# Moving the last merge's loads, the rotary rotation and the routing scores in a diffusion trunk on one Trainium2 core

## What is computed

```python
h = rmsnorm(x, g_pre1) * (1.0 + sc1) + sh1          # sh, sc, g: from silu(c) @ w_ada + b_ada
dq, dk, dv, sz, sxbc, sdt, nq, nk, nv = split_in(h @ w_in)
o_da = diff_attention(apply_axial_rope(dq), concat([ck, apply_axial_rope(dk)]), concat([cv, dv]), lam)
o_ssm = ssm_branch(...)                              # a state space branch
o_na = neighbourhood_attention(nq, nk, nv, ...)
ga, gs, gn = split(sigmoid(h @ w_gate), 3)
mix = (ga * (o_da @ w_br_da) + gs * (o_ssm @ w_br_ssm) + gn * (o_na @ w_br_na)) @ w_out
x = x + g1 * rmsnorm(mix, g_post1)
h2 = rmsnorm(x, g_pre2) * (1.0 + sc2) + sh2
s = sigmoid(h2 @ w_router)                           # 32 experts, the best 4 of a token are taken
x = x + g2 * rmsnorm(moe_ffn(h2), g_post2)           # routed experts and one shared expert

def rot_half(x, cos, sin):                           # on halves of 32: 16 frequencies for the row, 16 for the column
    x1, x2 = split(x, 2)
    return concat([x1 * cos - x2 * sin, x2 * cos + x1 * sin])
```

## Time and profile before

| | us |
|---|---|
| median of 3 runs | 2616.13 |
| lowest and highest | 2613.88, 2620.17 |
| the profiled execution | 2614.22 |
| its span | 2612.5 |
| PE busy | 2406.2 |
| DVE busy | 949.7 |
| ACT busy | 629.8 |
| POOL busy | 403.7 |

### The profile page before, as it was taken

The page is one execution under the profiler, slowest core; times in us unless marked ns, Lnnn a source line. Parts: engine busy times, 40 slices in busy tenths (PEclk is TensorE's granted clock), DMA queues, the critical chain, the costliest instruction groups (busy, mean ns, idle before and its releaser), DMA issues. The chain is left out here.

```text
span 2612.5 us, 36229 instructions
## 1 busy us (share of the span) xinstructions
PE 2406.2 (92%) x13804; PEld 1439.5 (55%) x13804; DVE 949.7 (36%) x1850; ACT 629.8 (24%) x1519; POOL 403.7 (15%) x456
## 2 busy tenths in 40 slices
PE   5999999989999999899779999998999999989995
PEld 2445644466557655555445565545655765555552
DVE  1423411473106423522364143137410642452226
ACT  2223401350015003122132252016001510312221
POOL 0003100021002300133410030000300230013333
PEclk7999999999999999899879999999999999999998
DMA  8443146100544030589653221220022403155985
GB/s 318 160 162 122 65 149 224 43 1 33 169 145 115 33 125 23 200 332 405 241 218 125 86 94 40 84 73 1 33 89 81 129 33 110 39 204 207 377 343 215
DMA packets 170173, 368.55 MB, mean 141 GB/s; under 512 B 38564, under 2 KB 52140, under 8 KB 170036
## 3 DMA queue, kind: packets, MB, share of 16 engines
q1 hardware_dynamic: 121876, 261.49, 27.4%
q10 hardware_dynamic: 24480, 54.76, 6.0%
q0 software_dynamic: 23680, 50.43, 5.9%
HBM read 344.19 MB, written 47.56 MB: 150 GB/s over the span
## 5 line engine op out<-in xcount | busy, mean ns | idle before, releaser
L228 PE MATMUL ps<-hT,ring 128*128 128x512 f32 x512 | 230.9, 605 | 6.3 <-PEq L1147 2.7
L2513 PE MATMUL ps<-ring,mixT 128*32 128x256 f32 x2688 | 214.0, 382 | 2.9 <-DMA ring<-in_w_e_up 2.5
L237 PE MATMUL ps<-ring,hT 128*128 128x512 f32 x480 | 211.9, 598 | 5.1 <-PEq L1191 4.1
L2513 PEld LDWEIGHTS ps<-ring,mixT 128*32 128x32 f32 x2688 | 120.3, 111 | 95.7 <-issue 21.8
L228 PEld LDWEIGHTS ps<-hT,ring 128*128 128x128 f32 x512 | 96.7, 193 | 130.4 <-issue 130.2
L237 PEld LDWEIGHTS ps<-ring,hT 128*128 128x128 f32 x480 | 90.5, 192 | 115.5 <-issue 113.6
L1278 PE MATMUL ps<-late,ring 128*128 128x320 f32 x512 | 147.2, 447 | 7.6 <-PEq L1366 3.9
L2391 PE MATMUL ps<-ring,mixT 128*128 128x512 f32 x320 | 142.1, 603 | 9.2 <-DVE out_xn L2680 4.8
L1278 PEld LDWEIGHTS ps<-late,ring 128*128 128x128 f32 x512 | 99.6, 196 | 52.9 <-issue 14.8
L1229 POOL TENSOR_TENSOR mix_S<-ring 128x512 f32<-128x512 f32 x16 | 25.2, 1577 | 651.1 <-POOLq L1366 550.1
L664 PE MATMUL ps<-hT,ring 128*128 128x512 f32 x256 | 114.5, 601 | 2.9 <-ACT ssm_dec L916 2.9
(11 more groups left out here) (475 smaller groups left out, 4164.1 us busy)
## 6 DMA issues: line engine op xcount, KB each, us to landing
ring<-in_w_in SPq DMA_DIRECT2D x18, 2048.0 KB, 9.8
ring<-in_w_gate SPq DMA_DIRECT2D x12, 2048.0 KB, 10.1
ring<-in_w_e_down SPq DMA_DIRECT2D x48, 512.0 KB, 17.2
ring<-in_w_e_gate SPq DMA_DIRECT2D x40, 512.0 KB, 5.3
ring<-in_w_e_up SPq DMA_DIRECT2D x40, 512.0 KB, 6.6
co_yg<-y_rows SPq DMA_DIRECT2D x40, 512.0 KB, 5.3
mixT<-in_w_ada ACTq DMA_DIRECT2D x8, 2048.0 KB, 8.7
da_ada_w<-in_w_ada ACTq DMA_DIRECT2D x8, 2048.0 KB, 8.8
```

The source lines that it names most:

```text
L228: pe.matmul(lat, wide[:, k, c], hT[:, k, CTX:TOK], start=(k == 0), stop=(k == kt_n - 1))
L237: last = pe.matmul(out, cx.hT[:, k, tok(t)], wide[:, k, :], start=(k == 0), stop=(k == KT - 1))
L2513: ins = pe.matmul(ps[rows, 2 + b, 0:2 * P].rearrange("p (g f) -> p g f", g=2), xT[:, b, k, rows], ew[:, :, k, :], start=(k == 0), stop=(k ...
```

## The change

- Rotary: the matrix `cx.rot` and its matmuls are gone. DVE shuffles the partitions itself (`stream_shuffle` with `HALF_TURN`, which exchanges the halves of each 32), and the sign is in the sine table. DVE waits for ACT's copy of the chunk (`da_lat_out`).
- Loads: `x`, the gate rows and both sets of modulation parts are allocated before the last merge (`m.post`, `m.own_mods`, `m.mods`) and loaded by SP at the start of it, ahead of the ring sections; SP waits for them at the end of that block. `stage_tail` loads bias and gain only. `stage_combine` uses `m.post` as two of its eight row buffers.
- Scores: the router columns are the stationary side, 32 wide, in four column groups side by side (k and k + 4 in one group); 128 tokens move. ACT copies the four partial sums (`router_out`), and a matmul with a constant `fold` adds them and turns them back (`router_fold`); the fold of a tile stands at the next tile's scores, that of the last behind its `rows_low`.

The diff, without the lines that only rename buffers in `stage_combine` and the constants in `trunk`:

```diff
@@ -48,6 +48,7 @@
 MASKED = -1.0e30
+HALF_TURN = [(i + 16) % 32 for i in range(32)]
...
@@ -122,7 +117,8 @@
         ang[p] = at * inv[d % 16]
-    rope = np.concatenate([np.cos(ang), np.sin(ang)], axis=1).astype(np.float32)
+    sign = np.where(t % 32 < 16, -1.0, 1.0)[:, None]
+    rope = np.concatenate([np.cos(ang), sign * np.sin(ang)], axis=1).astype(np.float32)
     mask = np.zeros((P, NBLK, NKEY), np.float32)
...
@@ -1179,7 +1175,7 @@
-def stage_mix(nc, cx, L, n, branch, g0):
+def stage_mix(nc, cx, L, n, branch, g0, m=None, x=None):
...
@@ -1217,7 +1213,19 @@
         @block.sync
         def _(sp):
+            if x is not None:
+                for g in range(2):
+                    sp.dma_start(m.post[:, g, :], cx.gate_rows[L, 0, g:g + 1, :].broadcast_to([P, D])).then_inc(
+                        name("gate_in"), 16)
+                load_x(cx, sp, L, x, name("x_in"))
+                load_mods(cx, sp, L, 1, m.own_mods, name("mods_in"))
+                if L + 1 < DEPTH:
+                    load_mods(cx, sp, L + 1, 0, m.mods, name("mods_in"))
             load_behind(cx, sp, L, ("gate", g0), ("gate", g0 + 1))
+            if x is not None:
+                sp.wait_ge(name("gate_in"), 32)
+                sp.wait_ge(name("x_in"), 32)
+                sp.wait_ge(name("mods_in"), 160 if L + 1 < DEPTH else 80)
         @block.gpsimd
...
@@ -1440,12 +1448,6 @@
                     pe.wait_ge(sem("da_mm"), n + 1)
                     pe.sem_inc(cx.ring_free, 1)
-                if n >= 2:
-
-                    src = (qT if n - 2 < 4 else kT)[:, (n - 2) % 4, -LAT:]
-                    if n >= 4:
-                        pe.wait_ge(sem("da_sin"), n - 3)
-                    pe.matmul(ps[:, 4 + n % 2, :], cx.rot, src, start=True, stop=True).then_inc(sem("da_rot"), 1)
                 if n == 7:
                     ada.fold(pe, 6)
...
@@ -1497,12 +1499,6 @@
                     ada.fold(pe, 7)
-                if t < 2:
-                    n = 8 + t
-                    pe.wait_ge(sem("da_lat_out"), n - 1)
-                    pe.wait_ge(sem("da_sin"), n - 3)
-                    pe.matmul(ps[:, 4 + n % 2, :], cx.rot, kT[:, n - 6, -LAT:], start=True, stop=True).then_inc(
-                        sem("da_rot"), 1)
                 if t == 0:
...
@@ -1674,9 +1670,10 @@
             def rope_chunk(n):
                 x = (qT if n < 4 else kT)[:, n % 4, -LAT:]
-                dve.wait_ge(sem("da_rot"), n + 1)
+                dve.wait_ge(sem("da_lat_out"), n + 1)
                 r = rt[:, n % 2, :]
-                dve.tensor_tensor(r, ps[:, 4 + n % 2, :], rope[:, 1, :], ALU.mult).then_inc(sem("da_sin"), 1)
+                step(dve, dve.stream_shuffle(r, x, HALF_TURN))
+                dve.tensor_tensor(r, r, rope[:, 1, :], ALU.mult)
                 step(dve, dve.tensor_tensor(x, x, rope[:, 0, :], ALU.mult))
                 dve.tensor_tensor(x, x, r, ALU.add).then_inc(sem("da_roped"), 1)
...
@@ -2208,9 +2205,9 @@
         xn = m.rest
-        mods = Mods(sb("out_mods", [P, 184]))
+        mods = m.own_mods
         ms = sb("out_ms", [P, 6, TILES])
-        gpost = sb("out_gpost", [P, 2, D])
+        gpost = m.post
         shsilu = sb("route_silu", [P, TOK])
...
@@ -2268,11 +2265,8 @@
         def _(sp):
-            load_gate(cx, sp, L, 0, gpost, xn[:, 3, :], xn[:, 4, :], sem("gate_in"))
-            load_x(cx, sp, L, x, sem("x_again"))
-            load_mods(cx, sp, L, 1, mods, sem("mods_in"))
-            if L + 1 < DEPTH:
-                load_mods(cx, sp, L + 1, 0, m.mods, sem("co_mods_in"))
+            sp.dma_start(xn[:, 3, :], w["b_ada"][L:L + 1, 2 * D:3 * D].broadcast_to([P, D])).then_inc(sem("gate_in"), 16)
+            sp.dma_start(xn[:, 4, :], w["g_post1"][L:L + 1].broadcast_to([P, D])).then_inc(sem("gate_in"), 16)
             sp.dma_start(wr[:, :, :], w["w_router"][bass.ds(L, 1)].rearrange("l (p k) n -> p (l k) n", k=KT)).then_inc(
...
@@ -2404,12 +2398,21 @@
                 if t == 0:
                     pe.wait_ge(sem("router_in"), 48)
+                else:
+                    router_fold(t - 1)
                 pe.wait_ge(sem("h_low"), t + 1)
                 pe.wait_ge(sem("h_high"), t + 1)
                 for k in range(KT):
-                    ins = pe.matmul(ps[:, 7, t * NE:(t + 1) * NE], cx.hT[:, k, tok(t)], wr[:, k, :], start=(k == 0),
-                                    stop=(k == KT - 1))
+                    j = k % 4
+                    ins = pe.matmul(ps[NE * j:NE * j + NE, 7, 3 * P:4 * P], wr[:, k, :], cx.hT[:, k, tok(t)],
+                                    start=(k < 4), stop=(k >= 4))
                 ins.then_inc(sem("router_mm"), 1)
+
+            def router_fold(t):
+
+                pe.wait_ge(sem("router_parts"), t + 1)
+                pe.matmul(ps[:, 7, t * NE:(t + 1) * NE], hid[:, t % 2, :], cx.fold[:, 0:NE], start=True,
+                          stop=True).then_inc(sem("router_sums"), 1)
             def rows_low(t):
...
@@ -2462,6 +2465,7 @@
             rows_low(TILES - 1)
+            router_fold(TILES - 1)
             shared_ctx(1)
...
@@ -2569,6 +2573,13 @@
+            def router_out(t):
+
+                act.wait_ge(sem("router_mm"), t + 1)
+                if t >= 2:
+                    act.wait_ge(sem("router_sums"), t - 1)
+                act.activation(hid[:, t % 2, :], ps[:, 7, 3 * P:4 * P], ACT.Copy).then_inc(sem("router_parts"), 1)
+
             for t in range(TILES):
...
@@ -2583,6 +2594,8 @@
                     modulate(t - 1)
+                if t >= 2:
+                    router_out(t - 2)
                 act.wait_ge(sem("x1_ready"), t + 1)
...
@@ -2591,7 +2604,9 @@
             rows_low(TILES - 2)
-            act.wait_ge(sem("router_mm"), TILES)
+            router_out(TILES - 2)
+            router_out(TILES - 1)
+            act.wait_ge(sem("router_sums"), TILES)
             act.activation(s[:, :, :].rearrange("p t e -> p (t e)"), ps[:, 7, 0:TILES * NE], ACT.Sigmoid).then_inc(
...
@@ -2663,16 +2678,14 @@
-            dve.wait_ge(sem("gate_in"), 64)
+            dve.wait_ge(sem("gate_in"), 32)
             finish_gate(cx, dve, gpost, xn[:, 3, :], xn[:, 4, :])
             ins.then_inc(sem("spare_rows"), 1)
-            dve.wait_ge(sem("mods_in"), 80)
             finish_mods(cx, dve, 1, mods).then_inc(sem("mods_known"), 1)
             dve.wait_ge(sem("mods_known"), 1)
-            dve.wait_ge(sem("x_again"), 32)
             for t in range(TILES):
...
@@ -3076,7 +3090,6 @@
             if more:
-                dve.wait_ge(sem("co_mods_in"), 80)
                 finish_mods(cx, dve, 0, m.mods).then_inc(sem("co_mods"), 1)
...
@@ -3213,15 +3226,18 @@
                 stage_na(nc, cx, L)
                 close_passed()
-                stage_mix(nc, cx, L, 1, "n", 4)
+                m = Cx()
                 x = mid.enter_context(nc.sbuf_tensor(f"x_{L}", [P, TILES, D], F32))
+                m.mods = Mods(mid.enter_context(nc.sbuf_tensor(f"next_mods_{L}", [P, 184], F32)))
+                m.own_mods = Mods(mid.enter_context(nc.sbuf_tensor(f"out_mods_{L}", [P, 184], F32)))
+                m.post = mid.enter_context(nc.sbuf_tensor(f"out_gpost_{L}", [P, 2, D], F32))
+                stage_mix(nc, cx, L, 1, "n", 4, m, x)
                 retire_half()
                 cx.half = ExitStack()
                 link = ExitStack()
-                for name in ("co_gains", "co_mods_in", "y_stored0", "y_stored1"):
+                for name in ("co_gains", "y_stored0", "y_stored1"):
                     cx.shared_sems[name] = link.enter_context(nc.semaphore(f"{name}_{L}"))
-                m = Cx()
                 m.hsh = mid.enter_context(nc.sbuf_tensor(f"shared_hidden_{L}", [P, 2, TOK], F32))
                 m.wsd = mid.enter_context(nc.sbuf_tensor(f"shared_down_{L}", [P, 2, D], F32))
```

## The result

The change brought the median from 2617.7 us (17 runs beside it) to 2597.75 us (17 runs, 2590.2 to 2616.0). The ratio is 0.9934, with a 95% interval of 0.992 to 0.9947: 17 us less, between 14 and 21; the plain difference of the medians is 19.9 us. I had forecast 2595 us, 21.1 us less than before, and a range of 2590.5 to 2601. Measured again later beside the last experiment, the ratio was 0.9925 (0.9907 to 0.9943).

A forecast was written before the change was run, and what follows sets the result against it. TensorE, busy 92% of the span, was taken as the bound. Rotary 12.3 + loads 7.6 + scores 1.2 = 21.1 us off the profiled 2614.2 gave 2593.1, forecast as a 2595 us median; range 2590.5 to 2601.

The forecast's parts named there:

- Rotary, second layer: Differential attention's projections, second layer: eight rotation matmuls removed at 0.86 us each, nothing else late; 6.9 us saved.
- Rotary, first layer: First layer's projections, where modulation-weight loads limit the gain: 5.4 us saved, bounds 1.7 and 6.9.
- the step with two transfers: First layer, load behind a ring section already holding PE 1.76 us: two rotations save 0 to 0.95, taken 0.5.
- Rival (a): First layer's transfers take back its rotations: 3.7 us less gain, 2599 us; chance 15%.
- Loads: Output projection's first tiles: earlier loads end PE's stops of 3.83 and 1.00 us and a slow clock; 7.6 us saved.
- its 2.72 us: First layer's output tiles: 16 instructions at granted clock 0.50 take 9.86 us instead of 7.14; 2.72 us saved.
- Scores: Routing scores packed in four column groups: 0.6 us a layer, 1.2 saved in all; bounds loss 2, gain 3.5.
- Shuffle: Added 128x512 shuffle a chunk on DVE in the projections: 0.69 us, hidden under PE, cost nothing.
- Rival (d): Shuffle bounds the projections from 6.3 us, eats the whole gain above 8.0; 2639 us at 10; chance 2%.
- rival (b): Bare table switch behind the score copies costs more than its row: 2.8 us less gain, 2598 us; chance 4%.
- Rival (c): Bias and gain rows still gate DVE, so PE stops at the tail as before: 7.6 us less, 2603; chance 6%.
- D: Follow-up theory on the missing 8 us: the change brings the slow clock, or moved loads slow work above them.

The follow-up runs named there:

- e2: Kernel before the change with the moved loads alone; 2611.3 us, ratio 0.9992.
- e3: Kernel before the change with the packed scores alone; 2614.0 us, ratio 0.9996.
- e12: Changed kernel measured once more, beside e11, nothing edited; 2598.5 us, ratio 0.9925 to the kernel before.
- e1: Kernel before the change with the rotary part alone (shuffle on VectorE, no rotation matmuls); 2602.2 us, ratio 0.9944.
- e4: Changed kernel with a one-column Sigmoid behind the output tiles' last square root, so the table loads there; 2600.1 us, ratio 0.9932.
- e9: Changed kernel; first layer's branch-weight ring section issued only after the eighth, last modulation-weight load has landed; 2595.95 us, ratio 0.9915.
- e10: e9 plus the early Sigmoid table of e4, with the last scores' fold ahead of four transposes on TensorE; 2590.9 us, ratio 0.9892.
- e11: e9 plus the early Sigmoid table of e4, last fold left where the change had it; 2589.9 us, ratio 0.9902.
- e5: Changed kernel; first layer's branch-weight ring section issued only after the sixth modulation-weight load has landed; 2600.2 us, ratio 0.9939.
- e6: Changed kernel with the early Sigmoid table of e4 and the later ring section of e5 together; 2594.5 us, ratio 0.9922.

## Why the prediction was right, and where it was not

The range held the time, and the middle missed by 2.8 us. Part of that nearness is luck: by the ratio the change saved 17 us where I had 21.1, and no term of mine knew of the slow starts behind gaps. Term by term, with all profiles that have the part:

**Rotary, second layer: 6.9 us forecast, 6.7 measured.** 109.20 to 109.24 us in all kernels with the plain shuffle, 115.92 to 115.95 in those without. The 0.2 is not one wait: the 0.30 us hand-over at the fifth chunk stands in before too. By pitch four of the eight rotations gave 0.85 to 0.86 us and one 0.94, but three only 0.78, since the row behind a hand-over takes 0.08 us longer and is now a projection or a value tile.

**Rotary, first layer: 5.4 forecast, 3.3 measured; this is the step that failed.** From the second product of modulation weights, ahead of all eight rotations, to the unit scores: 117.41, 117.15 and 117.40 us without the shuffle (before, e2, e3); 113.74, 113.86, 113.73 and 114.85 with it (after, e12, e1, e4). That is 117.3 against 114.0, 2.3 to 3.7 from pair to pair. For the step with two transfers I took half of the 0.95 us; the two took 14.5 us as before, so nothing was saved there. What I had not reckoned at all was the clock: the stop at this product was 1.48 to 1.76 us and is now 3.24 to 3.62, and each of these was followed by a slow product, 3.09 to 3.64 us instead of 1.92, which gave back up to 1.7 us more. This was also one of the prediction's own signs of being wrong, a lower clock in a place where it was full before. Rival (a) named the cause and priced the stage at 1.7 us; the measured 3.3 lies between it and my 5.4. With the section out of the way (e9, e10, e11: 108.50, 108.72, 109.07) the whole of the rotations comes through: 117.3 - 108.8 = 8.5 us, against 6.9 for them and 1.76 for the stop of before. These are single executions; the timed runs are too wide to show it alone.

**Loads: 7.6 forecast, 6.0 measured.** The mechanism was right, the stop is gone in all 22 places and nothing new is late. Mis-sized is the clock: its 2.72 us, and a term that I had at nothing. I read it from one execution as the price of the long stop; of the three profiles with the stop in the first layer only before's had it (its stop was 3.83 us, the others' 2.47 and 2.60 with full clock behind). Means over the table: first layer 39.7 with the stop, 35.0 without; second 36.8 and 35.5. That is 4.7 and 1.3, 6.0 us in all, uncertain by the few executions with the stop. Against 34.4 us, full clock and no stop, the stops cost 5.3 and 2.4 us, 7.7 together, about what I forecast though in other shares than my 6.55 and 1.00. The missing 1.7 are the slow starts, 0.6 and 1.1 us as means: while PE stopped for DVE anyway, the stop ended 31.5 to 32.0 us behind the first instruction of the first layer's output tiles whether they began slow (e1, e3) or not (before). With the stop gone, a slow start costs its full 1.7 us.

**Scores: 1.2 forecast, 1.8 measured.** The stretch to the mask products fell by 0.9 us in each layer of after, and stayed in e1 (59.45 and 59.49). In the second layer the first three tiles gave 0.77, 0.77 and 0.11 where I had 0.7, 0.66 and 0.1: 16 packed products have a pitch of 0.71 us, not 0.8. The fourth and the last lost 0.74 together, not 0.85, since the last fold lay under the table load. The sigmoid came 2.31 us behind the last scores, inside the 1.9 to 2.9 that I named.

**Shuffle: 0.69 taken, 0.72 measured, hidden.** The Trainium skill's figure ("VectorE: DVE Perf Modes", section "The perf-mode tier table") of about 2400 ns for 2048 elements led to an estimate of 0.7 for 512, and the trace agrees with its 0.72. Rival (d) was priced at a wrong place: it does not bind each step from 6.3 us on, up to twelve shuffles (9.2 us) the debt gathers behind the last chunk, and seven shuffles, 5.0 us in all, already cost 5.0 us in the second layer (nothing in the first, whose steps are longer by the products).

**Table load.** In e4 it is 1.28 us and the next ACTIVATE starts 0.01 us later, so rival (b) falls. The Trainium skill, "ScalarE: Activation LUTs", section "What ACT_TABLE_LOAD costs", adds a drain of about 1380 ns to each switch; the trace disagrees again, with that 0.01 us. Rival (c) fell with a room of 9 us: the accumulator is free at 2203.98, and PE asks for it at about 2213.

Sum: 6.7 + 3.3 + 6.0 + 1.8 = 17.8 us, inside the timed 14 to 21. So D, as a loss anywhere else in the kernel, can be a few microseconds at most. The profiled pair shows 13.0 because after's execution had the slower value at four places where before's had the faster (1.57 and 1.69 in the first layer, 1.75 on the second layer's way to its output tiles and some 1.4 from the mask products to the first expert), against 1.40 us that its start gained. The mean clock fits this, without showing the places: over the 17 timed runs the span and the granted clock go together (correlation -0.88, about 20 us for 0.01), and the profiled one stood at 0.962 and 3.5 us above the median span. The three parts timed alone give 14.6, 2.1 and 1.0 us as middles, 17.7 together, each by 3 to 5 us uncertain, so nothing is seen to be won or lost between them.

Left open: why the clock behind a gap takes one value or the other, whether a kernel can lean to one of them, and whether e10's loss is the fold's place in every execution. Not run: the later section on the kernel before, which would tell how much of e9's 5.2 us it gives without the change.

## What to carry to other kernels

Read a term of 1 to 2 us from several profiles, never from one pair: a stretch of steady work that begins behind a gap of TensorE can take 1.7 us more or less by the clock alone, and its own length, from first start to next start, tells which. A stop on the way can hide such a slow start, and then removing the stop gives less than its length. When TensorE's work beside a stream of transfers is removed, look at which step has two transfers in flight: there the removal lengthens the wait (1.76 to 3.56 us here), and moving the transfer that nobody waits for yet sets the gain free (e9: 5.2 us, on top of the 3.3 that the eight rotations had given). An instruction that gets slower on an engine with idle time in every step need not show in the step; its debt can surface behind the last one.

## What the runs showed of the hardware that I had not expected

- The same 80 matmuls of 128x512 behind the same 2.0 to 2.2 us gap took 34.4 or 36.1 us (34.88 or 36.57 in neighbourhood attention), with nothing between; the difference is a few microseconds at a granted clock of 0.50.
- A single stop of 2.47 to 2.60 us was followed by full clock in three cases (e1, e3 and e5), one of 2.11 us by a product of 2.67 us instead of 1.92 (e6) and one of 2.10 us by 16 instructions in 8.83 us instead of 7.14 (e3, second layer). So the length of one stop doesn't tell alone.
- Two waits of 1.02 and 0.40 us close together, among short transposes, were followed by a clock of 0.55 to 0.60 in both layers of e10, and without the second of them the clock stayed at 1.00 in e4. In e2's first layer it fell to 0.50 near that place while PE was busy without a gap of 0.1 us.
- Sixteen matmuls over four column groups, 128 columns each, took 0.71 us, 44 ns an instruction; the shuffle of 128x512 fp32 took 0.72 us.
